# Values projected ahead of the keys, attention's first scores between the key blocks, adaLN's last group within the values

## What is computed

```python
def trunk_layer(x, cond, lp, attend):
    sh1, sc1, gt1, sh2, sc2, gt2 = ada_mod(cond, lp['w_ada'], lp['b_ada'])
    h = rms_norm(x, lp['norm1_g']) * (1.0 + sc1) + sh1
    q, k, v, hy = split_projection(h @ lp['w_in'])
    att = attend(q, k, v)
    hyo = hyena_mixer(hy, lp)
    merged = jnp.concatenate([rms_norm(att, lp['gnorm_att']), rms_norm(hyo, lp['gnorm_hyena'])], axis=-1)
    x = x + gt1 * (merged @ lp['w_out'])
    h2 = rms_norm(x, lp['norm2_g']) * (1.0 + sc2) + sh2
    x = x + gt2 * hier_moe(h2, lp)
    return x, k, v
```

## Time and profile before

| | us |
|---|---|
| median of 3 runs | 757.82 |
| the profiled execution | 756.85 |
| its span | 755.1 |
| TensorE busy | 708.1 (94%) |
| VectorE busy | 535.3 (71%) |
| ScalarE busy | 411.7 (55%) |
| POOL busy | 109.5 (15%) |
| granted TensorE clock, mean | 0.974 |

### The profile page before, as it was taken

How to read it: one execution, slowest core, us unless ns; L and a number is a source line. 1 busy time by engine, 2 the same in 40 slices (tenths; PEclk the granted TensorE clock), 3 DMA queues, 4 the chain that set the end, 5 groups by cost and what they waited for, 6 DMA issues and landing times.

```text
span 755.1 us, 10721 instructions
## 1 busy us (share of the span) xinstructions
PE 708.1 (94%) x3842; PEld 536.3 (71%) x3842; DVE 535.3 (71%) x837; ACT 411.7 (55%) x623; POOL 109.5 (15%) x165
## 2 busy tenths in 40 slices
PE   5899999989999989999999389999999999999994
PEld 2368898949999855555554268888888888888863
DVE  3463616299633026666656888999999999999997
ACT  4762532341233024545542476888888888877933
POOL 2000000000033007554221100111111111111000
PEclk9999999999999989999999689999999999999998
DMA  8991135032368559700019888999999999999663
GB/s 325 417 391 59 66 158 195 3 139 96 141 142 230 227 197 392 194 2 29 2 46 361 289 325 289 351 369 378 380 384 393 388 372 398 384 367 378 237 254 142
DMA packets 81442, 186.73 MB, mean 247 GB/s; under 512 B 9140, under 2 KB 19540, under 8 KB 78196
## 3 DMA queue, kind: packets, MB, share of 16 engines
q1 hardware_dynamic: 73188, 167.10, 60.7%
q0 software_dynamic: 6448, 16.86, 6.8%
q10 hardware_dynamic: 1760, 2.17, 0.9%
HBM read 173.63 MB, written 18.38 MB: 254 GB/s over the span
## 4 chain that ended last, share of the span: by engine, by line
PE 84%; DVE 7%; DMA 4%; SPq 2%; ACT 2%; issue 2%; ACTq 0%; POOLq 0%; DVEq 0%
PE bank L2054 55%; PE bank L1947 13%; PE bank L1956 6%; DMA slot<-in_w_ada 3%; PE bank L1967 2%; PE bank L2208 2%; PE bank L2186 1%; PE bank L2179 1%; DVE WL L1751 1%; PE bank L2017 1%; DVE big L1885 1%; SPq L653 1%; DVE big L1895 1%; DVE big L1890 1%; PE bank L2004 1%
## 5 line engine op out<-in xcount | busy, mean ns | idle before, releaser
L1751 DVE TENSOR_TENSOR WL<-slot,WH 128x1024 fp32r<-128x1024 f32 x188 | 219.2, 1220 | 8.6 <-ACT WH L1205 7.7
L1205 ACT CAST WH<-slot 128x1024 fp32r<-128x1024 f32 x188 | 183.5, 1058 | 1.4 <-PE bank L2054 1.4
L2054 PE MATMUL bank<-WH,xgTh 128*128 128x512 f32 x256 | 102.6, 401 | 3.1 <-DVE xgTl L1743 3.1
L2054 PE MATMUL bank<-WH,xgTl 128*128 128x512 f32 x256 | 101.2, 395 | 0.0
L2054 PE MATMUL bank<-hTh,WP 128*128 128x384 f32 (+1 forms) x320 | 99.8, 312 | 0.0
L2054 PE MATMUL bank<-hTl,WP 128*128 128x384 f32 (+1 forms) x320 | 98.7, 308 | 0.0
L2054 PE MATMUL bank<-hTh,WL 128*128 128x384 f32 (+1 forms) x320 | 98.7, 308 | 0.0
L2054 PE MATMUL bank<-WL,xgTh 128*128 128x512 f32 x248 | 97.2, 392 | 0.0
L1947 PE MATMUL bank<-slot,big 128*128 128x512 f32 (+1 forms) x224 | 87.7, 539 | 0.1
L1956 PE MATMUL bank<-ident,big 128*128 128x128 f32 x424 | 61.3, 285 | 6.8 <-DMA big<-h_scratch,big 4.8
L1947 PEld LDWEIGHTS bank<-slot,big 128*128 128x128 f32 x224 | 40.9, 190 | 35.1 <-issue 33.1
(11 more groups left out here) (282 smaller groups left out, 1082.2 us busy)
## 6 DMA issues: line engine op xcount, KB each, us to landing
slot<-in_w_down SPq DMA_DIRECT2D x16, 2048.0 KB, 15.7
slot<-in_w_up SPq DMA_DIRECT2D x15, 2048.0 KB, 16.4
slot<-in_w_gate SPq DMA_DIRECT2D x13, 2048.0 KB, 16.1
slot<-in_w_ada SPq DMA_DIRECT2D x12, 2048.0 KB, 13.2
slot<-in_w_in SPq DMA_DIRECT2D x6, 2048.0 KB, 21.5
y_scratch<-dftp SPq DMA_DIRECT2D x1, 5120.0 KB, 40.2
big<-y_scratch SPq DMA_DIRECT2D x10, 512.0 KB, 7.5
slot<-in_w_out SPq DMA_DIRECT2D x2, 2048.0 KB, 14.7
```

The source lines that it names most:

```text
L1205: act.copy(WH[:, high_half(w, s), r, :], quarter(n, s, w, r)).then_inc(high_ok[w], 1)
L1751: dve.tensor_tensor(quarter_low(n, s, w, r), quarter(n, s, w, r), WH[:, high_half(w, s), r, :].bitcast(F32), ALU.subtract).then_inc(low_ok ...
L2054: ins = pe.matmul(out, l[u], r[v], start=first and i == 0, stop=last and i == 2)
```

## The change

1. **Load order.** The values' weights take the keys' place in `LOADS`, the keys' weights go behind `ada(2, 1)`, into slot 1; `ada(2, 2)` moves to slot 3. The high parts change homes with them, and Hyena's scratch `t1` moves out of the values' way.
2. **TensorE order.** Behind `ada(2, 0)` stand `ada(2, 1)`, value tiles 0 and 1, `ada(2, 2)`, value tiles 2 to 4, `hst`, `ada(2, 3)`. Key blocks 0 and 1 stand in step -1, block 2 in step 0, block 3 in step 1, each ahead of the scores of its step; the turned new keys stand behind the scores in step 1.
3. **The other engines** follow: ScalarE splits the keys' weights between its value copies, takes Hyena's square root before it waits for adaLN's last group, and copies key blocks within the attention steps. POOL loads gt1 in step 1, ahead of G2 and SH2, behind the last key pair; SP loads x again behind it too. VectorE's wait for gt1 moves to the first weighted sum.

```diff
+KEYS_IN = {-1: (0, 1), 0: (2,), 1: (3,)}
+NEW_KEYS_STEP = 1
...
     for v in range(-1, STEPS):
+        for cb in KEYS_IN.get(v, ()):
+            add(("k", cb), "act", 4 + cb % 2)
+            if cb % 2:
+                add(("kp", cb // 2), "act", 6)
         if v + 1 < PAIRS * NT:
             for u in heads(v + 1):
                 add(("s", u), "dve", u % 2)
+        if v == NEW_KEYS_STEP:
+            add(("nk",), "act", 6)
...
-         (("win", WQ), 1), (("tables",), 3), (("ada", 1, 3), 2), (("win", WK), 2), (("ada", 2, 0), 1), (("win", WV), 1),
-         (("ada", 2, 1), 3), (("ada", 2, 2), 2), (("ada", 2, 3), 3), (("wout", 0), 1), (("wout", 1), 2)]
+         (("win", WQ), 1), (("tables",), 3), (("ada", 1, 3), 2), (("win", WV), 2), (("ada", 2, 0), 1), (("ada", 2, 1), 3),
+         (("win", WK), 1), (("ada", 2, 2), 3), (("ada", 2, 3), 3), (("wout", 0), 2), (("wout", 1), 1)]
...
-            full(sp, "V", NT - 1)
+            full(sp, "kp", 1)
             sp.dma_start(x, a["x"].rearrange("(t p) n -> p t n", p=P)).then_inc(in_x, 16)
...
-            have(pool, "kp", 1)
-            pool.wait_ge(m_out[0], 64)
-            for c in range(2):
-                rows_of(gt1[:, c, :], c, 2, gt1_in)
             for v in range(-1, STEPS):
                 if v == 1:
-                    have(pool, "V", NT - 1)
+                    have(pool, "kp", 1)
+                    pool.wait_ge(m_out[0], 64)
+                    for c in range(2):
+                        rows_of(gt1[:, c, :], c, 2, gt1_in)
                     pool.wait_ge(m_out[1], 64)
...
             for t in range(NT):
                 b = full(act, "V", t)
                 drain(act.copy(V[:, t, :], b[:, :]), "V", t)
-            b = full(act, "nk")
-            drain(act.copy(nkb, b[:, :]), "nk")
-            have(act, "nk")
+                if t < 4:
+                    win_high(act, 5, t)
+            have(act, "V", NT - 1)
             act.dma_start(outs["v"], V[:, CT, :]).then_inc(kv_out, 16)
-            act.dma_start(outs["k"], nkb).then_inc(kv_out, 16)
+            act.wait_ge(hrt, 1)
+            act.activation(ss[:, 6, :], ss[:, 5, :], ACT.Sqrt, scale=1.0 / CH, bias=epsb[:, :]).then_inc(hy_rt, 1)
             act.wait_ge(g2_done, 1)
             store_rows(2)
...
             for v in range(-1, STEPS):
+                for cb in KEYS_IN.get(v, ()):
+                    turned_out("k", KTt, 1.0, cb)
                 if v + 1 < PAIRS * NT:
                     for u in heads(v + 1):
                         exps(u)
+                if v == NEW_KEYS_STEP:
+                    bk = full(act, "nk")
+                    drain(act.copy(nkb, bk[:, :]), "nk")
+                    have(act, "nk")
+                    act.dma_start(outs["k"], nkb).then_inc(kv_out, 16)
...
                 bk = full(dve, *f)
+                if i == 1:
+                    dve.wait_ge(gt1_in, 32)
...
             ada(2, 0)
-            project(("k",), ("kp",), 4)
             ada(2, 1)
+            for t in range(NT):
+                b = open_bank("V", t)
+                close(split_group(b[:, :], [(input_parts(k, t * P, (t + 1) * P), win_parts(4, k, 0, 512))
+                                            for k in range(KT)], 4 if t == 0 else None))
+                if t == 1:
+                    ada(2, 2)
 
             b = open_bank("hst")
             pe.wait_ge(hsum_ok, 1)
...
-            for t in range(NT):
-                b = open_bank("V", t)
-                close(split_group(b[:, :], [(input_parts(k, t * P, (t + 1) * P), win_parts(5, k, 0, 512))
-                                            for k in range(KT)], 5 if t == 0 else None))
-            ada(2, 2)
             ada(2, 3)
...
             for v in range(-1, STEPS):
+                for cb in KEYS_IN.get(v, ()):
+                    project_block(("k",), ("kp",), 5, cb)
                 if v + 1 < PAIRS * NT:
                     scores(v + 1)
+                if v == NEW_KEYS_STEP:
+                    new_keys()
```

More of the change, by code:

```diff
@@ L165, in psum_jobs @@
     add(("ada", 1), "dve", 7)
[L166 to L176, removed]
+    for cb in range(CB):
+        add(("q", cb), "act")
+        if cb % 2:
+            add(("qp", cb // 2), "act")
+    for cb in range(CB):
+        add(("inv", cb), "dve")
+    add(("invp",), "dve")
     for t in range(NT):
         add(("V", t), "act")
+    add(("hst",), "dve")
     add(("ada", 2), "dve", 7)
-    add(("nk",), "act")
     for v in range(-1, STEPS):
+        for cb in KEYS_IN.get(v, ()):
+            add(("k", cb), "act", 4 + cb % 2)
+            if cb % 2:
+                add(("kp", cb // 2), "act", 6)
         if v + 1 < PAIRS * NT:
@@ L242 @@
 ESLOT = [1, 2, 0, 3, 4, 5]
-PROJ = [(w, CHUNK[("win", w)]) for w in HY + [WQ, WK, WV]]
+PROJ = [(w, CHUNK[("win", w)]) for w in HY + [WQ, WV, WK]]
 WIN_KB = [[167, 171, 133.5, 125], [182, 186, 190, 194], [167, 171, 140, 178],
-          [188, 192, 167, 171], [178, 182, 188, 192], [0, 4, 8, 12]]
+          [188, 192, 167, 171], [0, 4, 8, 12], [178, 182, 188, 192]]
 HYROW = range(3)
@@ L347, in program @@
         sq = at(167, CB, TOK)
-        t1 = at(0, 2, TOK)
+        t1 = at(178, 2, TOK)
         QT, KTt = at(134.75, CB, TOK), at(124.5, CB, TOK)
@@ L1074, in _, with turned_out @@
             act.wait_ge(sets_ok, 1)
[L1075 to L1082, removed]
+            def turned_out(ch, dst, scale, cb):
+                b = full(act, ch, cb)
+                drain(act.activation(dst[:, cb, 0:FRONT], b[:, 0:FRONT], ACT.Copy, scale=scale), ch, cb)
+                if cb % 2:
                     b = full(act, ch + "p", cb // 2)
@@ L1085, in _ @@
                                          scale=scale), ch + "p", cb // 2)
[L1086 to L1096, removed]
+            for cb in range(CB):
+                turned_out("q", QT, -DH ** -0.5, cb)
+            act.wait_ge(y_ok, 3)
+            for r in range(4):
+                win_high(act, 4, r)
+            have(act, "ada", 1)
+            store_rows(1)
+            load_bias(2)
+            act.dma_start(g2row, a["g2r"]).then_inc(g2row_in, 16)
+            hyena_gain()
+            have(act, "invp")
+            act.dma_start(cv, a["cv"]).then_inc(in_ctx, 16)
             for t in range(NT):
@@ L2071, in input_parts, with project_block @@
                 return hTh[:, k, lo:hi], hTl[:, k, lo:hi]
+            def project_block(job, jobp, c, cb):
+                rest = TOK - FRONT
+                weights = [win_parts(c, k, cb * P, (cb + 1) * P) for k in range(KT)]
+                b = open_bank(*job, cb)
+                close(split_group(b[:, 0:FRONT], [(weights[k], input_parts(k, 0, FRONT)) for k in range(KT)],
+                                  c if cb == 0 else None))
+                bp = open_bank(*jobp, cb // 2)
+                ins = split_group(bp[:, cb % 2 * rest:(cb % 2 + 1) * rest],
+                                  [(weights[k], input_parts(k, FRONT, TOK)) for k in range(KT)])
+                if cb % 2:
+                    close(ins)
             def project(job, jobp, c):
-                rest = TOK - FRONT
                 for cb in range(CB):
[L2077 to L2085, removed]
+                    project_block(job, jobp, c, cb)
             def project_first():
@@ L2156, in _, with new_keys @@
             close(ins)
[L2157 to L2170 removed]
+            ada(2, 3)
+            def new_keys():
+                have(pe, "kp", 1)
+                b = open_bank("nk")
+                for cb in range(CB):
+                    ins = turn(b[:, cb * P:(cb + 1) * P], KTt[:, cb, LAT:TOK])
+                close(ins)
             def scores(v):
@@ L2174, in scores @@
                 kts = key_tiles(b)
+                if b == 0:
+                    have(pe, "k", pair)
+                elif v == PAIRS:
+                    have(pe, "kp", 1)
                 for u in heads(v):
```

11 lines of the change are left out of this document (1 added, 10 removed).

## The result

The changed kernel takes 769.71 us (median, 768.46 to 770.85) and the kernel before, run beside it, 758.34 us (757.72 to 759.27). The ratio is 1.0157, with a 95% interval of 1.0137 to 1.0177: 11.4 us slower. The prediction was 770.0. The profiled execution took 770.85 us, with a span of 769.1.

What follows compares the result with a forecast made beforehand. TensorE was taken to bound the kernel. Second wait 16.3 plus clock 2.2 minus gain 6.3 gave +12.2 on the profiled 756.85, so 769.1; the median standing 0.97 above made 770.0, range 765 to 776.

Steps and rivals of the forecast that it cites:

- gain at the first scores: From the end of the values to step 1's transposes, 6.3 us can go, hole and half clock together.
- quarter 3 and the keys: Quarter 3 issued at 244, read at 262; key weights land near 238, block 0 starts near 265: no cost.
- rows and x late: After the last key pair, POOL's row loads and SP's x come late: taken as 0, up to 5 us.
- Second wait: TensorE, behind value tile 1, waits for adaLN quarter 2 to land at 242 instead of 225.7: 16.3 us.
- on SP's queue the key weights stand ahead of it: SP's queue serves in order, so quarter 2 follows the key weights and lands near 242, bounds 239 to 245.
- First wait: TensorE, behind adaLN quarter 0, waits for quarter 1 from 212.95 to 218: 5.1 us, lying within the time to 242.
- Clock: Half clock behind the new hole before 242 costs 2.2 us, ends 1.2 and 2.7.
- so 7.1 us of TensorE work cover it: Key blocks 2 and 3 behind the first and second scores cover step 0's softmax of about 3 us.
- The rival that each of steps 2 to 5 waits: Rows and x lack slack: 3 to 8 us more, 773 to 778; chance 0.17 together with no cover.
- the key blocks did cover the first scores: Its rival: key blocks fail to cover the first softmax, up to 5 us back, 775; 0.17 together with rows late.
- full-rate rival: Bias rows slow nothing, all loads from 209.5 are down near 229 to 231: no change, 757 to 759; chance 0.05.
- Faster: Quarter 2 lands below 230 to 232, so the change gains at most 2.4 us, 755.4; chance 0.03.

Runs made afterwards that it cites:

- experiment 1: Changed kernel with adaLN quarter 1 used behind value tile 1, quarter 2 behind tile 4, quarter 3 behind key block 0; 751.11 us, 0.9926 of before.
- Experiment 4: Changed kernel with POOL's eight position bias loads held back until quarter 2 has landed; 758.49 us, 1.0016 of before.
- experiment 6: Changed kernel with all four key blocks ahead of the first scores; 771.12 us, 1.019 of before.
- kernel 7: Kernel of experiment 1 with all four key blocks ahead of the first scores; 754.65 us, 0.9968 of before.
- Experiment 8: Kernel before, ScalarE's order alone: Hyena root ahead of value copies, two output and four row stores behind the first exponentials; 757.63 us, 1.0009.
- experiment 9: Kernel before, ScalarE's order alone: Hyena root ahead of value copies, only the output stores behind the first exponentials; 756.71 us, 0.9988.
- experiment 2: Kernel of experiment 1 with quarter 3 alone put back behind the Hyena sums; 760.43 us, 1.0055 of before.
- experiment 3: Kernel of experiment 1 with quarter 1 alone put back directly behind quarter 0; 760.55 us, 1.0041 of before.
- experiment 5: Kernel of experiment 1 with the position bias loaded only after quarter 2 has landed; 754.02 us, 0.9957 of before.

## Why the prediction was right

| term, us | predicted | measured |
|---|---|---|
| gain at the first scores | 6.3 | 6.15 (in after); 5.55 (experiment 1) |
| landing of quarter 1 | 218 (from 209.5, 8.5) | 219.88 (from 210.15, 9.7) |
| first hole | 5.1 | 6.16 |
| landing of quarter 2 | 242, issued 219.9 | 242.14, issued 223.6 |
| second hole | 9 to 11 | 7.27 |
| half clock, second hole | 2.2 | 2.95 |
| quarter 3 and the keys | 0 | 0 |
| rows and x late | 0, up to 5 | 0.84 |
| end of step 1 | 299.4 | 300.27 |
| time | 770.0 | 769.71 |

**Second wait.** Its cost, 16.3 us, hung on one number, 242, and that held to 0.2 us (to 0.6, counted from quarter 0, which began 0.75 us later in this execution than before; so the two holes with the first half clock cost 15.6). It held although quarter 2 was issued 3.7 us later than I put it (quarter 1 itself was late and took 3.64 us at half clock). That the step "on SP's queue the key weights stand ahead of it" carries the landing, and not the time of issue, is what this shows, and experiment 1 again: issued at 227.3, landed at 242.6. Experiment 4 shows the other half of the step, the bias rows: without them the wait is gone.

**First wait.** 6.16 against 5.1: the load took 9.7 us where I gave it 8.5. The mis-sized term is what the load takes beyond a quiet one; I charged 1.0 us for in_rpb, from a share of 24.6% in 214 to 218, and it was 1.8 to 2.4. Experiment 4 splits it: with the bias rows away the load still took 8.3, so they are 1.4 of the 9.7. SP issued it at 210.15, 0.65 us behind my 209.5, since in this execution the inverse transforms were that late. That the hole vanishes in the second held: the sum needed no term for it, and the measured 6.16 + 2.15 (half clock) + 7.27 + 2.95 = 18.5 us is the same amount as my 16.3 + 2.2, split in another way.

**Clock.** The term of 2.2 was too small. Behind the second hole a quarter and three value tiles took 3.64 + 17.57 us, where they take 1.85 + 16.41 at full clock: 2.95 us lost, over my upper end of 2.7. I had shrunk it from the nearest row, a hole of 2.86 us with a loss of 2.7, with no row that spoke for a smaller one.

**Gain.** 6.15 instead of 6.3 in after itself: from quarter 0 to the end of step 1 it takes 12.38 us more than before, 18.5 are holes and half clock, and the rest is gain. Experiment 1 has 5.55; its values, cut twice by a quarter, take 27.70 us instead of 27.35. So the size was right, but not quite for the reason that I gave. I put it all down to key blocks that cover the first softmax. Experiments 6 and 7 give these 2.5 to 2.6 us; kernel 7 keeps 3.03 us of gain with none between the scores. The step that failed in part is "so 7.1 us of TensorE work cover it": the hole of 2.86 was not the softmax's length but VectorE's first pass over the scores behind the root and the stores on ScalarE. Once these stood elsewhere 0.96 was left, and the clock stayed at 1.00. Experiment 8 confirms the cause (2.86 became 0.69) and gives its size up to the end of step 1: 2.53 us, against the 3.03 of kernel 7. In the kernel before it was given back by the late row stores, and experiment 9 had 1.13 of it because a second hole stayed. That the 2.53 are the same in the new order, and where the other 0.5 us come from, isn't shown.

**Rows and x.** I said VectorE "may stand 1 to 3 us, with 5 us of slack behind it"; it stood 5.97, so 0.84 us reached TensorE: from step 1's end to the router's first matmuls in step 9 pass 48.06 us in after, 47.22 before and in experiment 1. The slack was right and the wait too short: in experiment 2 VectorE stood 5.77 us there and TensorE lost 0.63, in experiment 3 5.42 and 0.28, in experiment 1 3.90 and nothing. The first three give 5.1 us of slack each, and experiment 1 lies within it. The rival that each of steps 2 to 5 waits (3 to 8 us) didn't come. Nor did the others: the DMA engines didn't run near full rate for the rest of the queue (1.39 MB on SP's in 16 us), quarter 2 was far from 230, and the key blocks did cover the first scores. The sum of the full-rate rival is wrong in itself: 230.5 + 23.2 + 1.5 + 34 is 289.2, not 288. With the 21.3 that stands in the rival "Faster" it is 287.3, level with 287.2, so the reading "no change" stands.

**Sum.** 18.53 (6.16 + 2.15 + 7.27 + 2.95) - 6.15 + 0.84 = 13.22, the distance. I had 12.2: the holes and the clock together are as I put them (18.5), with the wait 0.7 too long and the clock 0.75 too short, and the rest of the difference is the rows and 0.15 of the gain. The spans differ by 14.0 (0.75 of it ahead of quarter 0) and the medians by 11.4, so this pair of profiled executions lies some 2 us apart beyond what the runs show. The kernel before, run beside, also took 0.5 us more than the 757.82 from which I started. So 769.71 beside 770.0 is closer than the terms are, and that is luck; by the runs alone the change cost 11.4 where I said 12.2.

## What to carry to other kernels

When a piece of work is moved forward, ask for each load it reads when its slot is free, and what stands ahead of it on its queue; the landing, not the issue, sets the cost. Consumers are to be moved together with the places where they find their data: here the same change with three of its four quarters placed by their landings gains 6 us instead of losing 11. And before new cover is built over a stall, see what stands ahead of the stalled work on its own engine. Here another order on ScalarE removed most of the hole, and then the stores that it had put off had to be followed too, for they gave the gain back.

## What I had not expected of the hardware

- 1.57 MB of bias rows in eight loads (192 KB each) on POOL's queue slowed one 2,048 KB load on SP's queue from 10.6 us to 23.4 (experiment 4 against after). At the 405 GB/s of 234 to 240 they would take 4 us. But each queue had about half of the engines' time from 218 to 234, and together they moved only 2.78 MB in 16 us, 174 GB/s. The rows are as slow alone (130 GB/s with the engines fully busy, experiment 5), so most of the cost is their own and not that of two queues side by side. Each of these loads goes to 16 partitions (`NA_COLS`), where SP's go to 128, its packets are of 3 KB on average, and POOL issues it. Which of these makes them slow was not tried.
- Quarter 2 was issued 3.7 us later in experiment 1 than in after (227.3 against 223.6) and landed only 0.5 us later, since its queue decided.
- Stores of 4 KB took 7.41 us when they were issued among large transfers (experiment 8).
- Holes of 0.96, 0.33 and 0.18 us left TensorE's granted clock at 1.00 (experiment 6), and so did 1.46 and 0.33 us in a row (experiment 8, 292 to 295). A single hole of 2.09 us brought 0.50 (experiment 5), and so did 0.69 and 1.52 us within 4 us (experiment 9).
- Executions of code that is the same up to quarter 0 reach it up to 2.7 us apart (209.66 to 212.35).
